# The sparse attention's queries projected transposed: the weight block stationary, 256 tokens moving

## The chip, the core and the metric

The kernel runs on one NeuronCore of a Trainium2 chip. The metric is the device time of one execution in microseconds (us); lower is better. Engines: PE is TensorE's matmuls, PEld its weight loads (the loading of the stationary operand), DVE is VectorE, ACT ScalarE, POOL GpSimd, SP the engine that issues the transfers.

## The reference

One layer of a decoder trunk over 256 tokens of width 2048, all in float32: a pre-norm, one projection of 2048 to 18,776 columns, three token mixers, their gates, a branch projection and an output projection each, and a post-norm with the residual. What matters here is the third mixer:

```python
h = rmsnorm(x, pre_norm_g[l])
proj = jnp.einsum('bsd,dn->bsn', h, w_in[l])       # dsa_q: 8 heads x 256 columns of it
...
q = q.reshape(b, s, DSA_HEADS, DSA_LATENT)         # 8 x 256
c = rmsnorm(ckv, kv_norm_g)
...
logits = jnp.einsum('bqhc,bqkc->bqhk', qb, c_sel).astype(jnp.float32) * (DSA_LATENT ** -0.5)
p = jax.nn.softmax(jnp.where(valid[:, :, None, :], logits, -jnp.inf), axis=-1)
ob = jnp.einsum('bqhk,bqkc->bqhc', p.astype(c.dtype), c_sel)
return jnp.einsum('bqhc,hcv->bqhv', ob, w_uv)
```

The logits contract over the 256 latent columns, so on TensorE the queries have to stand with these columns on the partitions: transposed.

## The kernel before

**Products.** Each float32 operand of a big projection is split in two float32r parts, high and low, and a product is three matmuls: high by high, high by low, low by high. The input's parts are `xhi` and `xlo` (128 partitions of the width, 16 blocks `kt`, 256 tokens). The weights come in units of 256 rows by 512 columns: SP loads a unit into one of four slots of `raw`, ACT rounds it to `whi` (L559), DVE subtracts to get `wlo` (L822), PE multiplies. A unit frees its slot for the rounding of the fourth unit behind it. Eight units make a group of 512 output columns.

**`multiply` (L1223 to L1236).** A unit is 12 matmuls: 2 blocks `kt`, 2 blocks `t` of 128 tokens, 3 products. The stationary operand is 128 tokens of `xhi` or `xlo`, the moving one 512 weight columns; the result stands in two PSUM banks, tokens on the partitions, one bank for each `t`. `take_group` on ACT (L562) copies the two banks to `area0` or `area1` and scales each token by its `rstdx`, the pre-norm's factor, which is per partition there.

**Stages, by parts of the stream.** `PS` (small columns, 344 wide), `PA` (8 groups), `PB` (8), `PC` (4 turns of 2 groups), then per branch b a part `PP[b]` of 4 turns of 12 units (8 units of gates, 4 of the branch's projection), `PV` between `PP[0]` and `PP[1]`, and `PO` (4 groups of `w_out`). Turns 0 and 1 of `PC` are the 2048 columns of the sparse attention's queries: 4 groups, 32 units. The mixers' small operations stand at fixed units between the big ones in the same program: the mLSTM in `PC`, the sparse attention in `PP[1]`, two heads a turn, a head at 6 units.

**The order of a head of the sparse attention in `PP[1]`.** POOL copies the head's 256 query columns to `ya_blk`. After unit u = 0 PE transposes them, 4 transposes of 128x128 into `M[0]` (L1462), and ACT copies them to `dsa_qT` (L750). After u = 1 PE computes the logits in plain float32 (L1469: 4 matmuls, in the trace two passes each), and DVE scales them and adds the mask (L1142) and takes the maxima (L1145). ACT takes the exponential (L755) behind its rounding at u = 2, PE transposes the probabilities after u = 3 (L1475) and multiplies them by the values after u = 4 (L1483, L1485).

**Loops.** On each engine the turns of a part are a hardware loop (`Fori`); the units within a turn are written out. The last turn of `PP[2]` and the 32 units of `PO` are written out altogether. Order between engines is by semaphores that count up.

Of the kernel before, what the change touches and what calls it, by code (L numbers as in the profile page):

```python
# [34 lines left out]
ALU = mybir.AluOpType  # L35
# [3 lines left out]
P = 128  # L39
# [108 lines left out]
def build(nc, x, pre_norm_g, w_in, da_lambda, da_norm_g, ml_conv_w, ml_conv_b, ml_gate_b, ml_norm_g,  # L148
          dsa_kv_norm_g, dsa_ik_norm_g, dsa_w_uv, w_branch, w_out, post_norm_g, out):
    with ExitStack() as ctx:  # L150
# [52 lines left out]
        gate_in = tiny[:, 116:132].rearrange("p (t e) -> p t e", t=TILES)  # L203
        forget_t = tiny[:, 156:164].rearrange("p (t h) -> p t h", t=TILES)
        conv_h = tiny[:, 132:142].rearrange("p (a j) -> p a j", a=2)
        wait_carrier = tiny[:, 166:167]
        sqrt_first = tiny[:, 167:168]
        one = tiny[:, 142:143]
# [55 lines left out]
        idx_acc = view(scratch, 2048, 3 * P)  # L264
        select = view(scratch, 768, 3 * P)
        idx_relu = view(room1, 0, 2, 3 * P)
        dsa_q = ya_blk[:, :, :]
        dsa_qT = view(room0, 512, 2, SEQ)
        dsa_pT = view(room1, 512, 3 * P)
        dsa_s = view(scratch, 1152, 3 * P)  # L270
        dsa_sig = view(scratch, 1536, TILES, P)
# [52 lines left out]
                                                          sem("iw_fetched"))  # L324
        idx_fetched, idx_T_psum, iqT_ready = sem("idx_fetched"), sem("idx_T_psum"), sem("iqT_ready")
        idx_scores, idx_relu_ready, idx_added = sem("idx_scores"), sem("idx_relu_ready"), sem("idx_added")
        dsa_fetched, dsa_T_psum, dsa_qT_ready = sem("dsa_fetched"), sem("dsa_T_psum"), sem("dsa_qT_ready")
        dsa_logits, dsa_negmax, dsa_exp = sem("dsa_logits"), sem("dsa_negmax"), sem("dsa_exp")
        dsa_pT_psum, dsa_pT_ready = sem("dsa_pT_psum"), sem("dsa_pT_ready")
        chi_ready, clo_ready, v_taken = sem("chi_ready"), sem("clo_ready"), sem("v_taken")  # L330
# [107 lines left out]
        def _(pool):  # L438
# [92 lines left out]
                fetch_iw(p * 2 + (IW0 + 2))  # L531


            pool.wait_ge(idx_T_psum, IDX_HEADS // 2)
            nc.gpsimd.tensor_copy(dsa_q, area0[:, :, 0:DSA_LATENT]).then_inc(dsa_fetched, 1)
            with pool.Fori(0, DSA_HEADS - 1) as h:
                pool.wait_ge(dsa_T_psum, h + 1)
                nc.gpsimd.tensor_copy(dsa_q, area0[:, :, bass.ds(h * DSA_LATENT + DSA_LATENT, DSA_LATENT)]  # L538
                                      ).then_inc(dsa_fetched, 1)


            pool.wait_ge(end_landed, 48)
            for n, (t, columns) in enumerate(FINAL_POOL):
                pool.wait_ge(y_scaled, n + 1)
# [5 lines left out]
        def _(act):  # L550
# [11 lines left out]
            def take_group(part, i, k_end, bank_pair, to, width=GROUP):  # L562

                act.wait_ge(units_done, part.unit(i, k_end))
                for t in range(TILES):
                    nc.scalar.activation(to[t], stream[bank_pair][t][:, 0:width], ACT.Copy, scale=rstdx[:, t:t + 1]  # L566
                                         ).then_inc(banks_free, 1)

            act.wait_ge(cols_turned, 1)
            nc.scalar.activation(cols[:, :], M[0][:, 0:56], ACT.Copy).then_inc(cols_ready, 1)  # L570
# [88 lines left out]
            nc.scalar.activation(da_ss, da_ss, ACT.Sqrt).then_inc(da_std, 1)  # L659


            with act.Fori(0, PC.turns) as i:
                for v in range(2 * FULL_UNITS):
                    round_unit(PC, i, v)
                    if v == 1:
                        act.wait_ge(ml_T_psum, i + 1)
                        nc.scalar.activation(ml_xT[:, :, ML_CONV - 1:], M[0][:, :].rearrange("p (a s) -> p a s", a=2),
                                             ACT.Copy).then_inc(ml_xT_ready, 1)
                    if v == 4:
                        act.wait_ge(ml_conv, i + 1)  # L670
                        nc.scalar.activation(ml_sT, ml_cT, ACT.Tanh, scale=0.5).then_inc(ml_ts, 1)
                        act.wait_ge(ml_arg, i * 2 + 2)
                        nc.scalar.activation(ml_E, ml_E, ACT.Exp).then_inc(ml_exp, 1)
                    if v == 11:
                        act.wait_ge(ml_gated, i + 1)
                        nc.scalar.activation(ml_to, area1[:, :, bass.ds(i * ML_V + 2 * WIDTH, ML_V)], ACT.Tanh,
                                             scale=0.5).then_inc(ml_toz, 1)
                        nc.scalar.activation(ml_tz, area1[:, :, bass.ds(i * ML_V + 3 * WIDTH, ML_V)], ACT.Tanh,
                                             scale=0.5).then_inc(ml_toz, 1)
                    if v == 3:  # L680
                        act.wait_ge(ya_psum, i + 1)
                        nc.scalar.activation(yhi[:, bass.ds(i * 2, 2), :],
                                             M[2][:, :].rearrange("p (k s) -> p k s", k=2), ACT.Copy
                                             ).then_inc(yhi_ready, 1)
                    if v in (FULL_UNITS - 1, 2 * FULL_UNITS - 1):
                        g = v // FULL_UNITS
                        take_group(PC, i, (g + 1) * FULL_UNITS, (PC.group0 + g) % 2,
                                   [area0[:, t, bass.ds(i * 2 * GROUP + g * GROUP, GROUP)] for t in range(TILES)])
# [54 lines left out]
            with act.Fori(0, PP[1].turns) as i:  # L743
                for v in range(PAIR_UNITS):
                    round_unit(PP[1], i, v)
                    s, u = v // 6, v % 6
                    h = i * 2 + s
                    if u == 0:
                        act.wait_ge(dsa_T_psum, h + 1)
                        nc.scalar.activation(dsa_qT, M[0][:, :].rearrange("p (c s) -> p c s", c=2), ACT.Copy  # L750
                                             ).then_inc(dsa_qT_ready, 1)
                    if u == 2:
                        act.wait_ge(dsa_negmax, h * 2 + 2)
                        for t, a, n in ((0, 0, P), (1, P, 2 * P)):
# [58 lines left out]
        def _(dve):  # L813
# [60 lines left out]
            steps.step(nc.vector.tensor_tensor(neglam, lam2[:, 1:2], lam2[:, 0:1], ALU.subtract))  # L874
            steps.step(nc.vector.tensor_scalar(neglam, neglam, LAM_INIT, None, ALU.subtract))

            dve.wait_ge(kv_squared, 2)
            steps.step(nc.vector.tensor_reduce(sskv[:, 0:2], kv_sq, AX.X, ALU.add))
            steps.step(nc.vector.tensor_reduce(sskv[:, 2:4], ik_sq, AX.X, ALU.add))
# [254 lines left out]
            with dve.Fori(0, PP[1].turns) as i:  # L1134
                steps.enter(i, 2 * 4)
                for v in range(PAIR_UNITS):
# [2 lines left out]
                    h = i * 2 + s  # L1139
                    if u == 1:  # L1140
                        dve.wait_ge(dsa_logits, h + 1)
                        steps.step(nc.vector.scalar_tensor_tensor(dsa_s, M[1][:, 0:3 * P], DSA_LATENT ** -0.5, select,  # L1142
                                                                  ALU.mult, ALU.add))
                        for t, a, n in ((0, 0, P), (1, P, 2 * P)):
                            nc.vector.tensor_reduce(dsa_negmax_c[:, t:t + 1], dsa_s[:, a:a + n], AX.X, ALU.max,  # L1145
                                                    negate=True).then_inc(dsa_negmax, 1)
# [74 lines left out]
        def _(pe):  # L1221
            def multiply(part, i, k, u, units, bank_pair, left_hi, left_lo, width=GROUP):

                slot = (part.unit0 + k) % RING
                pe.wait_ge(wlo_ready, part.unit(i, k) + 1)
                for j in range(UNIT_KT):
                    kt = UNIT_KT * u + j
                    first, final = kt == 0, kt == UNIT_KT * units - 1
                    for t in range(TILES):
                        to = stream[bank_pair][t][:, 0:width]  # L1230
                        tokens = slice(t * P, (t + 1) * P)
                        high, low = whi[:, slot, j, 0:width], wlo[:, slot, j, 0:width]
                        nc.tensor.matmul(to, left_hi[:, kt, tokens], high, start=first, stop=False)  # L1233
                        nc.tensor.matmul(to, left_hi[:, kt, tokens], low, start=False, stop=False)  # L1234
                        last = nc.tensor.matmul(to, left_lo[:, kt, tokens], high, start=False, stop=final)  # L1235
                last.then_inc(units_done, 1)  # L1236

            def open_banks(part, i, k):
# [103 lines left out]
            last.then_inc(rows_turned, 1)  # L1342


            with pe.Fori(0, PC.turns) as i:
                for v in range(2 * FULL_UNITS):
                    g, u = v // FULL_UNITS, v % FULL_UNITS
                    if u == 0:
                        open_banks(PC, i, g)
                    multiply(PC, i, v, u, FULL_UNITS, (PC.group0 + g) % 2, xhi, xlo)  # L1350
# [23 lines left out]
                    if v == 10:  # L1374
# [6 lines left out]
                        nc.tensor.matmul(M[3][:, 0:n], ml_w[:, P:2 * P], ml_v[:, 0, :], start=True, stop=False)  # L1381
                        nc.tensor.matmul(M[3][:, 0:n], ml_w[:, 2 * P:], ml_v[:, 1, :], start=False, stop=True
                                         ).then_inc(ml_num, 1)

            def gate_units(part, i, v, n0):

# [59 lines left out]
            pe.wait_ge(v_taken, 2)  # L1446


            with pe.Fori(0, PP[1].turns) as i:
                for v in range(PAIR_UNITS):  # L1450
                    s, u = v // 6, v % 6
                    h = i * 2 + s
# [1 line left out]
                        gate_units(PP[1], i, v, 4)  # L1454
                    else:
                        branch_units(PP[1], i, v, 4, 9)
                    if u == 0:
                        pe.wait_ge(dsa_fetched, h + 1)
                        pe.wait_ge(ylo_ready, 9)
                        for c in range(2):  # L1460
                            for t in range(TILES):
                                last = nc.tensor.transpose(M[0][:, c * SEQ + t * P:c * SEQ + (t + 1) * P],  # L1462
                                                           dsa_q[:, t, c * P:(c + 1) * P], ident[:, :])
                        last.then_inc(dsa_T_psum, 1)
                    if u == 1:
                        pe.wait_ge(dsa_qT_ready, h + 1)
                        for t, a, n in ((0, 0, P), (1, P, 2 * P)):
                            for c in range(2):
                                last = nc.tensor.matmul(M[1][:, a:a + n], dsa_qT[:, c, t * P:(t + 1) * P],  # L1469
                                                        cT[:, c, 0:n], start=(c == 0), stop=(c == 1))  # L1470
                        last.then_inc(dsa_logits, 1)
                    if u == 3:
# [84 lines left out]
```

## Time and profile before

| | before |
|---|---|
| device time, 3 runs | median 1133.67 us (1132.83 to 1134.2) |
| span of the profiled execution | 1131.5 us |
| PE busy, matmuls | 1110.0 us, 98% of the span |
| PEld busy | 915.0 us, 81% |
| DVE, ACT, POOL busy | 657.7, 549.5, 70.8 us |
| chain that ended last | 95% on PE |
| mean granted clock of TensorE | 0.995 of full speed |

The span runs from the first to the last instruction; of the profiled execution it is the only time there is, and the median of the timed runs is 2.2 us above it. A PE record lasts longer than the engine needs for it: records of matmuls that follow each other overlap, so the distance from start to start is what a matmul costs. The start of a weight load coincides with the start of the matmul before it, so starts of weight loads tell when matmuls begin.

### The profile page before, as it was taken

Reading aid. Unit: us, or ns where it says so; the run is one execution under the profiler, and the core shown is the slowest. Engines: PE = TensorE matmul, PEld = TensorE weight load, DVE = VectorE, ACT = ScalarE, POOL = GpSimd, SP = SyncE. Lnnn points to the kernel's source line nnn. Section 1 sums busy time; section 2 is a strip of 40 time slices with the busy share of each in tenths; the row PEclk is TensorE's granted clock in tenths of the full one; section 3 lists DMA queues with packets and bytes.
Section 4 is the critical chain, followed back from the end, with each engine's and each line's share of the span. In section 5 each row is a group of like instructions: output and inputs, shape, how many; then the busy total and the mean of one; then the engine's idle time right before and its main releaser. Section 6 shows DMA issues by size and latency. Waiting matters only on the chain.

```text
span 1131.5 us, 15625 instructions
## 1 busy us (share of the span) xinstructions
PE 1110.0 (98%) x5143; PEld 915.0 (81%) x5143; DVE 657.7 (58%) x910; ACT 549.5 (49%) x736; POOL 70.8 (6%) x122
## 2 busy tenths in 40 slices
PE   7999999999999999999999999999999999999995
PEld 6788888888878888888887778888888888888884
DVE  4744444666566676665766566665556645556454
ACT  6644444555454554544546444454444544445442
POOL 1000000100100011120210000000000000000001
PEclk9999999999999999999999999999999999999998
DMA  8666666566556546666556556655555476676551
GB/s 245 223 190 192 197 188 197 173 170 183 167 169 175 167 140 184 192 180 184 169 168 192 164 157 191 205 167 163 166 163 160 129 222 191 197 238 229 196 195 75
DMA packets 112399, 205.09 MB, mean 181 GB/s; under 512 B 11064, under 2 KB 15728, under 8 KB 111984
## 3 DMA queue, kind: packets, MB, share of 16 engines
q1 hardware_dynamic: 112368, 204.70, 60.1%
q8 instruction: 17, 0.28, 0.1%
q14 instruction: 14, 0.11, 0.0%
HBM read 202.57 MB, written 2.10 MB: 181 GB/s over the span
## 4 chain that ended last, share of the span: by engine, by line
PE 95%; SPq 2%; DVE 1%; ACT 1%; issue 0%; DMA 0%; DVEq 0%; ACTq 0%
PE stream L1233 30%; PE stream L1235 30%; PE stream L1234 29%; SPq L367 1%; PE mixer L1469 1%; DVE area L1216 1%; DVE wlo L822 0%; PE mixer L1496 0%; PE mixer L1485 0%; PE mixer L1328 0%; PE mixer L1303 0%; PE mixer L1404 0%; PE mixer L1462 0%; PE mixer L1429 0%; PE mixer L1314 0%
## 5 line engine op out<-in xcount | busy, mean ns | idle before, releaser
L822 DVE TENSOR_TENSOR wlo<-raw,whi 128x1024 fp32r<-128x1024 f32 (+1 forms) x378 | 460.9, 1222 | 430.5 <-ACT whi L559 428.5
L559 ACT ACTIVATE whi<-raw 128x1024 fp32r<-128x1024 f32 (+1 forms) x378 | 397.7, 1054 | 553.6 <-PE stream L1235 537.9
L1233 PE MATMUL stream<-whi,xhi 128*128 128x512 f32 (+1 forms) x1312 | 518.6, 395 | 2.8 <-DVE wlo L822 2.4
L1235 PE MATMUL stream<-whi,xlo 128*128 128x512 f32 (+1 forms) x1312 | 510.1, 389 | 0.0
L1234 PE MATMUL stream<-wlo,xhi 128*128 128x512 f32 (+1 forms) x1312 | 509.0, 388 | 0.0
L1233 PEld LDWEIGHTS stream<-whi,xhi 128*128 128x128 f32 x1312 | 246.8, 188 | 56.6 <-issue 5.8
L1235 PEld LDWEIGHTS stream<-whi,xlo 128*128 128x128 f32 x1312 | 246.6, 188 | 51.6
L1234 PEld LDWEIGHTS stream<-wlo,xhi 128*128 128x128 f32 x1312 | 247.1, 188 | 48.1
L1233 PE MATMUL stream<-whi,yhi 128*128 128x512 f32 x192 | 77.1, 401 | 0.0
L1235 PE MATMUL stream<-whi,ylo 128*128 128x512 f32 x192 | 75.0, 391 | 0.0
L1234 PE MATMUL stream<-wlo,yhi 128*128 128x512 f32 x192 | 74.8, 390 | 0.0
L1235 PEld LDWEIGHTS stream<-whi,ylo 128*128 128x128 f32 x192 | 36.0, 188 | 7.8
L1233 PEld LDWEIGHTS stream<-whi,yhi 128*128 128x128 f32 x192 | 36.1, 188 | 7.6 <-issue 0.7
L1234 PEld LDWEIGHTS stream<-wlo,yhi 128*128 128x128 f32 x192 | 36.1, 188 | 7.1
L566 ACT ACTIVATE area<-stream,tiny 128x512 f32 x48 | 30.0, 675 | 0.0
L468 POOL COPY mixed<-area 128x256 f32 (+1 forms) x24 | 10.7, 467 | 193.7 <-ACT area L566 173.6
L546 POOL TENSOR_TENSOR area<-area 128x512 f32<-128x512 f32 x3 | 5.0, 1696 | 261.6 <-ACT area L808 261.6
L538 POOL COPY ya_blk<-area 128x512 f32 x7 | 4.3, 612 | 190.8 <-PE mixer L1462 190.8
L697 ACT ACTIVATE area<-stream,tiny 128x512 f32<-128x512 f32 x24 | 15.0, 677 | 0.0
L472 POOL TENSOR_TENSOR mixed<-mixed 128x256 f32<-128x256 f32 x8 | 4.9, 614 | 159.2 <-DVE mixed L954 159.2
L637 ACT ACTIVATE mixed<-mixed,tiny 128x128 f32<-128x128 f32 (+1 forms) x32 | 14.1, 441 | 0.0
L513 POOL TENSOR_TENSOR mixed<-mixed 128x512 f32<-128x512 f32 x4 | 7.8, 1953 | 87.4 <-DVE mixed L1031 87.4
(244 smaller groups left out, 567.9 us busy)
## 6 DMA issues: line engine op xcount, KB each, us to landing
raw<-in_w_in SPq DMA_DIRECT2D x288, 512.0 KB, 3.7
raw<-in_w_branch SPq DMA_DIRECT2D x48, 512.0 KB, 4.5
raw<-in_w_out SPq DMA_DIRECT2D x32, 512.0 KB, 3.7
mixed<-in_x SPq DMA_DIRECT2D x4, 512.0 KB, 6.0
raw<-in_w_in SPq DMA_DIRECT2D x8, 256.0 KB, 3.9
area<-in_x SPq DMA_DIRECT2D x2, 1024.0 KB, 9.2
out<-area SPq DMA_DIRECT2D x8, 256.0 KB, 2.3
raw<-in_dsa_w_uv SPq DMA_DIRECT2D x4, 256.0 KB, 3.0
```

The source lines that it names most:

```text
L367: sp.dma_start(raw[:, slot, :, at:at + n], w_in_d[:, UNIT_KT * u:UNIT_KT * (u + 1), col:col + n]).then_inc(raw_landed[slot], 16)
L468: nc.gpsimd.tensor_copy((da_q, da_k, da_v)[n], area0[:, :, bass.ds(at + n * WIDTH, P)]).then_inc(da_v_fetched if n == 2 else da_fetched, 1)
L559: nc.scalar.activation(whi[:, slot, :, 0:width], raw[:, slot, :, 0:width], ACT.Copy).then_inc(whi_ready, 1)
L566: nc.scalar.activation(to[t], stream[bank_pair][t][:, 0:width], ACT.Copy, scale=rstdx[:, t:t + 1]).then_inc(banks_free, 1)
L637: nc.scalar.activation(da_s[:, c, a:a + n], da_s[:, c, a:a + n], ACT.Exp, bias=da_negmax_c[:, 2 * t + c:2 * t + c + 1], accum_out=da_sum_c ...
L697: nc.scalar.activation(sig[:, t, :], stream[part.group0 % 2][t][:, :], ACT.Tanh, scale=half_rstdx[:, t:t + 1]).then_inc(gate_tanh, 1)
L822: nc.vector.tensor_tensor(wlo[:, slot, :, 0:width], raw[:, slot, :, 0:width], whi[:, slot, :, 0:width].bitcast(F32), ALU.subtract).then_in ...
L1216: nc.vector.scalar_tensor_tensor(to, to, rstdo[:, t:t + 1], x_again[:, t, columns], ALU.mult, ALU.add).then_inc(y_dve, 1)
L1233: nc.tensor.matmul(to, left_hi[:, kt, tokens], high, start=first, stop=False)
L1234: nc.tensor.matmul(to, left_hi[:, kt, tokens], low, start=False, stop=False)
L1235: last = nc.tensor.matmul(to, left_lo[:, kt, tokens], high, start=False, stop=final)
L1469: last = nc.tensor.matmul(M[1][:, a:a + n], dsa_qT[:, c, t * P:(t + 1) * P], cT[:, c, 0:n], start=(c == 0), stop=(c == 1))
```

## The change

In turns 0 and 1 of `PC` the operands change places. A new `multiply_turned` takes 128 weight columns as the stationary operand and all 256 tokens as the moving one, so that the result stands transposed: latent columns on the partitions, tokens along the free axis. A unit is then 24 matmuls of 256 columns in place of 12 of 512. One bank holds one head, each half of it one block of 128 of its latent columns. `take_group` copies these banks unscaled (a token is no longer a partition), and `dsa_qT` is the copy in `area0` itself. The factor `rstdx` goes into the scaling of the logits on DVE, as `rstd_q` (with the 1/16 of the logits), one instruction for each block of tokens in place of one for both. POOL's copies to `ya_blk`, PE's transposes and ACT's copies for them go, with the three semaphores between them. On PE and ACT the body of `PC` is written out twice, for turns 0 and 1 and for turns 2 and 3, and PE's loop over the turns of `PP[1]` is written out.

```diff
+        rstd_q = tiny[:, 164:166]
...
-        dsa_q = ya_blk[:, :, :]
-        dsa_qT = view(room0, 512, 2, SEQ)
+        dsa_qT = [area0[:, h % 2, h // 2 * GROUP:(h // 2 + 1) * GROUP].rearrange("p (c s) -> p c s", c=2)
+                  for h in range(DSA_HEADS)]
...
-            pool.wait_ge(idx_T_psum, IDX_HEADS // 2)
-            nc.gpsimd.tensor_copy(dsa_q, area0[:, :, 0:DSA_LATENT]).then_inc(dsa_fetched, 1)
-            with pool.Fori(0, DSA_HEADS - 1) as h:
-                pool.wait_ge(dsa_T_psum, h + 1)
-                nc.gpsimd.tensor_copy(dsa_q, area0[:, :, bass.ds(h * DSA_LATENT + DSA_LATENT, DSA_LATENT)]
-                                      ).then_inc(dsa_fetched, 1)
...
-                    nc.scalar.activation(to[t], stream[bank_pair][t][:, 0:width], ACT.Copy, scale=rstdx[:, t:t + 1]
-                                         ).then_inc(banks_free, 1)
+                    nc.scalar.activation(to[t], stream[bank_pair][t][:, 0:width], ACT.Copy,
+                                         scale=1.0 if turned else rstdx[:, t:t + 1]).then_inc(banks_free, 1)
...
+            with act.Fori(0, 2) as i:
+                mlstm_turn(i, True)
+            with act.Fori(2, PC.turns) as i:
+                mlstm_turn(i, False)
...
-                    if u == 0:
-                        act.wait_ge(dsa_T_psum, h + 1)
-                        nc.scalar.activation(dsa_qT, M[0][:, :].rearrange("p (c s) -> p c s", c=2), ACT.Copy
-                                             ).then_inc(dsa_qT_ready, 1)
...
+            steps.step(nc.vector.tensor_scalar(rstd_q, rstdx, DSA_LATENT ** -0.5, None, ALU.mult))
             dve.wait_ge(kv_squared, 2)
...
-                        steps.step(nc.vector.scalar_tensor_tensor(dsa_s, M[1][:, 0:3 * P], DSA_LATENT ** -0.5, select,
-                                                                  ALU.mult, ALU.add))
+                        for t, a, n in ((0, 0, P), (1, P, 2 * P)):
+                            last = nc.vector.scalar_tensor_tensor(dsa_s[:, a:a + n], M[1][:, a:a + n],
+                                                                  rstd_q[:, t:t + 1], select[:, a:a + n],
+                                                                  ALU.mult, ALU.add)
+                        steps.step(last)
...
+            def multiply_turned(part, i, k, u, bank_pair):
+
+                slot = (part.unit0 + k) % RING
+                pe.wait_ge(wlo_ready, part.unit(i, k) + 1)
+                for j in range(GROUP // P):
+                    columns = slice(j * P, (j + 1) * P)
+                    to = stream[bank_pair][j // 2][:, j % 2 * SEQ:(j % 2 + 1) * SEQ]
+                    for c in range(UNIT_KT):
+                        kt = UNIT_KT * u + c
+                        high, low = whi[:, slot, c, columns], wlo[:, slot, c, columns]
+                        nc.tensor.matmul(to, high, xhi[:, kt, :], start=kt == 0 and j % 2 == 0, stop=False,
+                                         skip_group_check=True)
+                        nc.tensor.matmul(to, high, xlo[:, kt, :], start=False, stop=False, skip_group_check=True)
+                        last = nc.tensor.matmul(to, low, xhi[:, kt, :], start=False, stop=kt == KT - 1,
+                                                skip_group_check=True)
+                last.then_inc(units_done, 1)
...
-            with pe.Fori(0, PP[1].turns) as i:
+            for i in range(PP[1].turns):
...
-                    if u == 0:
-                        pe.wait_ge(dsa_fetched, h + 1)
+                    if u == 1:
                         pe.wait_ge(ylo_ready, 9)
-                        for c in range(2):
-                            for t in range(TILES):
-                                last = nc.tensor.transpose(M[0][:, c * SEQ + t * P:c * SEQ + (t + 1) * P],
-                                                           dsa_q[:, t, c * P:(c + 1) * P], ident[:, :])
-                        last.then_inc(dsa_T_psum, 1)
-                    if u == 1:
-                        pe.wait_ge(dsa_qT_ready, h + 1)
                         for t, a, n in ((0, 0, P), (1, P, 2 * P)):
                             for c in range(2):
-                                last = nc.tensor.matmul(M[1][:, a:a + n], dsa_qT[:, c, t * P:(t + 1) * P],
+                                last = nc.tensor.matmul(M[1][:, a:a + n], dsa_qT[h][:, c, t * P:(t + 1) * P],
                                                         cT[:, c, 0:n], start=(c == 0), stop=(c == 1))
```

## Rows read from the trace of the kernel before

**Rows 1.** The page: busy time of two engines, and the granted clock in 40 slices.

```profile
PE 1110.0 (98%) x5143; PEld 915.0 (81%) x5143; DVE 657.7 (58%) x910; ACT 549.5 (49%) x736; POOL 70.8 (6%) x122
PEclk9999999999999999999999999999999999999998
```

**Rows 2.** Waits of PE: who was waited for, us in total, times, longest.

```profile
PE stream L1233 <- DVE wlo L822: 2.4, 4, 1.2
```

**Rows 3.** Weight loads in order of time, 344 columns moving: start, duration; 40 records.

```profile
23.84 0.19 PEld L1235 LDWEIGHTS stream<-whi,xlo 128*128 128x128 f32 x1
...
29.82 0.19 PEld L1235 LDWEIGHTS stream<-whi,xlo 128*128 128x128 f32 x1
```

**Rows 4.** Weight loads, 512 columns moving: 12 records from 30.66, 36 from 33.21.

```profile
30.55 0.19 PEld L1233 LDWEIGHTS stream<-whi,xhi 128*128 128x128 f32 x1 [0.55 <-DVE wlo L822]
30.66 0.19 PEld L1234 LDWEIGHTS stream<-wlo,xhi 128*128 128x128 f32 x1
...
33.21 0.19 PEld L1233 LDWEIGHTS stream<-whi,xhi 128*128 128x128 f32 x1
...
41.14 0.19 PEld L1235 LDWEIGHTS stream<-whi,xlo 128*128 128x128 f32 x1
```

**Rows 5.** Weight loads around a head's transposes of the queries (L1462) in `PP[1]`.

```profile
744.04 0.59 PEld L1462 LDWEIGHTS mixer<-ident,ya_blk 128*128 128x128 f32 x4
...
744.71 0.19 PEld L1234 LDWEIGHTS stream<-wlo,xhi 128*128 128x128 f32 x1
```

**Rows 6.** Chain that ended last: the transposes of the first and the last of 8 heads.

```profile
744.43 0.44 PE mixer L1462 x4
...
879.09 0.44 PE mixer L1462 x4
```

**Rows 7.** Weight loads around the other three blocks of the first head.

```profile
747.23 1.29 PEld L1469 LDWEIGHTS mixer<-scratch,area 128*128 128x128 f32 x8
...
748.77 0.19 PEld L1234 LDWEIGHTS stream<-wlo,xhi 128*128 128x128 f32 x1
...
754.03 0.47 PEld L1475 LDWEIGHTS mixer<-ident,scratch 128*128 128x128 f32 x3
...
754.59 0.19 PEld L1234 LDWEIGHTS stream<-wlo,xhi 128*128 128x128 f32 x1
...
757.11 0.41 PEld L1483 LDWEIGHTS mixer<-area 128*128 128x128 f32 x2
757.45 0.53 PEld L1485 LDWEIGHTS mixer<-area 128*128 128x128 f32 x4
757.89 0.19 PEld L1233 LDWEIGHTS stream<-whi,xhi 128*128 128x128 f32 x1
758.00 0.19 PEld L1234 LDWEIGHTS stream<-wlo,xhi 128*128 128x128 f32 x1
```

**Rows 8.** Weight loads in `PO`, whose program is written out: 44 records.

```profile
1059.82 0.19 PEld L1233 LDWEIGHTS stream<-whi,xhi 128*128 128x128 f32 x1
...
1069.56 0.19 PEld L1234 LDWEIGHTS stream<-wlo,xhi 128*128 128x128 f32 x1
```

**Rows 9.** DVE and ACT around the new instruction's place: start, duration.

```profile
37.88 0.17 DVE L881 TENSOR_SCALAR tiny<-tiny 128x2 f32<-128x2 f32 x1
...
37.95 1.28 ACT L603 ACT_TABLE_LOAD   x1
39.24 0.21 ACT L603 ACTIVATE tiny<-tiny 128x4 f32<-128x4 f32 x1
```

**Rows 10.** DVE and ACT of the first head, between the logits and the exponential.

```profile
749.88 0.55 DVE L1142 SCALAR_TENSOR_TENSOR scratch<-mixer,scratch 128x384 f32<-128x384 f32 x1
750.47 0.61 DVE L1145 TENSOR_REDUCE tiny<-scratch 128x1 f32<-128x128 f32 x2
...
752.70 0.38 ACT L755 ACTIVATE scratch<-scratch,tiny 128x128 f32<-128x128 f32 x1
```

More of the change, by code:

```diff
@@ L326, in build @@
         idx_scores, idx_relu_ready, idx_added = sem("idx_scores"), sem("idx_relu_ready"), sem("idx_added")
-        dsa_fetched, dsa_T_psum, dsa_qT_ready = sem("dsa_fetched"), sem("dsa_T_psum"), sem("dsa_qT_ready")
         dsa_logits, dsa_negmax, dsa_exp = sem("dsa_logits"), sem("dsa_negmax"), sem("dsa_exp")
@@ L560, in round_unit, with take_group @@
                                      ).then_inc(whi_ready, 1)
-            def take_group(part, i, k_end, bank_pair, to, width=GROUP):
+            def take_group(part, i, k_end, bank_pair, to, width=GROUP, turned=False):
                 act.wait_ge(units_done, part.unit(i, k_end))
                 for t in range(TILES):
-                    nc.scalar.activation(to[t], stream[bank_pair][t][:, 0:width], ACT.Copy, scale=rstdx[:, t:t + 1]
-                                         ).then_inc(banks_free, 1)
+                    nc.scalar.activation(to[t], stream[bank_pair][t][:, 0:width], ACT.Copy,
+                                         scale=1.0 if turned else rstdx[:, t:t + 1]).then_inc(banks_free, 1)
             act.wait_ge(cols_turned, 1)
@@ L659, in _, with mlstm_turn @@
             nc.scalar.activation(da_ss, da_ss, ACT.Sqrt).then_inc(da_std, 1)
-            with act.Fori(0, PC.turns) as i:
+            def mlstm_turn(i, turned):
                 for v in range(2 * FULL_UNITS):
@@ L687, in _ @@
                         take_group(PC, i, (g + 1) * FULL_UNITS, (PC.group0 + g) % 2,
-                                   [area0[:, t, bass.ds(i * 2 * GROUP + g * GROUP, GROUP)] for t in range(TILES)])
+                                   [area0[:, t, bass.ds(i * 2 * GROUP + g * GROUP, GROUP)] for t in range(TILES)],
+                                   turned=turned)
+            with act.Fori(0, 2) as i:
+                mlstm_turn(i, True)
+            with act.Fori(2, PC.turns) as i:
+                mlstm_turn(i, False)
             act.wait_ge(ml_ms, 1)
@@ L1342, in _, with mlstm_turn @@
             last.then_inc(rows_turned, 1)
-            with pe.Fori(0, PC.turns) as i:
+            def mlstm_turn(i, turned):
                 for v in range(2 * FULL_UNITS):
@@ L1349, in _ @@
                         open_banks(PC, i, g)
-                    multiply(PC, i, v, u, FULL_UNITS, (PC.group0 + g) % 2, xhi, xlo)
+                    if turned:
+                        multiply_turned(PC, i, v, u, (PC.group0 + g) % 2)
+                    else:
+                        multiply(PC, i, v, u, FULL_UNITS, (PC.group0 + g) % 2, xhi, xlo)
                     if v == 1:
@@ L1383, in _ @@
                                          ).then_inc(ml_num, 1)
+            with pe.Fori(0, 2) as i:
+                mlstm_turn(i, True)
+            with pe.Fori(2, PC.turns) as i:
+                mlstm_turn(i, False)
             def gate_units(part, i, v, n0):
```

## The prediction

> **What bounds the kernel now.** First the page: PE is busy 98% of the span, DVE 58%, ACT 49%, and the granted clock is at its full level in all but the last slice [rows 1]. A busy PE is not yet a bound, so next the waits of PE: behind the start, all waiting for the rounded weights comes to 2.4 us in four places [rows 2]. PE is thus never starved from some 43 us on, and the time is the sum of what PE is given to do. What an operation costs there is not its record (0.19 us for a weight load) but the distance between starts. With 512 columns moving that is (41.14 - 33.21)/35 = 0.2266 us [rows 4], with 344 columns (29.82 - 23.84)/39 = 0.1533 us [rows 3]. The change is to be priced in such distances, all on PE.
>
> **What it removes on PE.** Eight blocks of four transposes. Around the first head's block, the matmul before it begins at 744.04 and the first matmul behind it at 744.71 (the load for the one after starts with it) [rows 5]. That is 0.67 us less one stream matmul: 0.443 us. The chain of work gives the same 0.44 [rows 6]. Eight of them: 3.54 us.
>
> A block also interrupts the stream, and that has a price of its own. Heads repeat every (879.09 - 744.43)/7 = 19.24 us [rows 6]. In this lie 72 stream matmuls, 72 x 0.2266 = 16.31, the logits 1.54 - 0.23 = 1.31, the transposes of the probabilities 0.56 - 0.23 = 0.33, and the product with the values 0.89 - 0.23 = 0.66 [rows 7], with the queries' 0.44 a total of 19.05. The missing 0.18 us lie behind the four interruptions, 0.045 each. One is seen after the wait at 30.55: for 11 matmuls the distance is 0.2318 before it settles at 0.2266, 0.057 in all [rows 4]. Eight interruptions fewer at 0.045: 0.36 us. Removed together: 3.9 us. From below, if the tails belong to the other blocks alone, 3.5; from above, with 0.057 each, 4.0.
>
> **What it adds on PE.** 32 units of 24 matmuls with 256 columns moving replace 32 of 12 with 512: 768 for 384. The old ones cost 384 x 0.2266 = 87.0 us. No row has a float32r matmul of 256 columns. Two limits stand for it.
>
> The moving side: through the rows at 344 and 512 the slope is 0.0733/168 = 0.436 ns a column with 3.4 ns left over, so 256 columns take 115.0 ns. Lower bound: the cost goes with the columns alone, as if no fixed part existed, 0.2266/2 = 113.3 ns. Upper bound: 344 columns at 2.4 GHz (the clock is at its upper level in these stretches) are 143.3 ns, so 10 ns lie over; if all of them are fixed, 106.7 + 10 = 116.7 ns.
>
> The weight side: the number of loads doubles, and each still loads 128 columns. How long does one really take? Behind the wait the load starts at 30.55 and its matmul at 30.66 [rows 4]: 0.11 us, with nothing else in the array. Behind the product with the values, which are passes of full 128x128 loads, the starts of the last five passes are 757.45 to 757.89, 0.11 each, and the stream's own first load takes until 758.00, again 0.11 [rows 7]. So a load can be repeated every 0.11 us, and 115 ns of matmul cover it, by only 5 ns. At 512 columns the cover was more than 100 ns.
>
> The Trainium skill ("TensorE: Matmul & The Clock Gate", section "LDWEIGHTS (loading the stationary operand)") has a load at its columns over 1.2, for 128 an estimated 107 ns whatever the rows; the trace's 0.11 agrees, and not the record's 0.19. The same page's "Back-to-back issue gap" gives load-and-matmul pairs sustained 81 ns at 128 columns and 131 at 512; a straight line between them is 98 at 256, two of which cost 64 ns more than one of 512, an estimate of 384 x 0.064 = 25 us against this change. The trace does not bear those figures out: its 512 columns take 227 ns, so I don't go by them; what they warn of is the second rival.
>
> I take 115.0 ns, the line through the two nearest rows: 768 x 0.1150 = 88.3 us, 1.3 us more than before. Bounds from the moving side: 87.0 (nothing) and 89.6 (2.6 more).
>
> **What costs nothing, and why.**
> - *The 16 interruptions of the mLSTM* in turns 0 and 1 of the projection stay where they are.
> - *The scale `rstd_q` on DVE*, early: one tiny operation like L881, 0.17 us and its step. DVE finishes L881 at 38.05, ACT is then loading a table until 39.23 and takes the root behind it at 39.24 [rows 9]. The 0.2 us fall into that 1.2. Without this cover the rounded weights, for which PE waits at this place [rows 2], would come 0.2 us later and so would the end.
> - *Two scalings of the logits in place of one*, some 0.2 us more for the second's overhead: L1142 ends at 750.43, the maxima near 751.1, and ACT's exponential starts at 752.70 behind its own rounding [rows 10]. 1.6 us cover it. Uncovered, the transposes of the probabilities, which PE begins one matmul after 754.03 [rows 7], would come late, by 8 x 0.2 = 1.6 us at most.
> - *ACT's and POOL's copies*, 16 in all: neither engine is waited for, so their going gives nothing. `take_group` has the same two copies with another scale.
> - *PE's wait for `ylo_ready`* goes from behind unit 0 to behind unit 1, a place later, with nothing queued ahead of it that it could hold.
> - *Written-out code*: in `PO`, where PE's program is written out, (1069.56 - 1059.82)/43 = 0.2265 us [rows 8], the same as in loops; and the eight starts of the transposes are evenly 19.24 us apart, whether the end of a turn lies between them or not [rows 6]. Neither a gain nor a loss.
> - *Transfers*: SP's list is the same, and no queue is moved past.
>
> **The sum.** -3.9 + 1.3 = -2.6 us. The profiled span of 1131.5 us becomes 1128.9; the median stands 2.2 us above that span, so 1133.67 - 2.6 = 1131.1 us, 0.23% less. What this kernel's measurement can tell from no change is about 0.2%, 2.3 us, so the forecast stands just over that line.
>
> **The rivals.**
> *First, a fixed part per matmul, still under the old time.* Price: 116 to 118 ns each, all fixed or with a few ns of the load uncovered. Speaks for it: the load's 0.11 us has only 5 ns of cover, and behind each interruption the stream runs 5 ns a matmul slower for a while [rows 4]. Time: 768 x 0.117 = 89.9, +2.9, so -1.0: 1132.7 us, no difference that can be told.
>
> *Second, the load becomes the bound.* If a load at 0.11 us has to hand over to its matmul with what a matmul of 512 columns has over its columns, 226.6 - 213.3 = 13.3 ns, the distance is 123.3 ns: 768 x 0.1233 = 94.7, +7.7, less 3.9 is +3.8: 1137.5 us, slower. It cancels the gain from 118.4 ns on, (87.0 + 3.9)/768, and is measurably slower from 121.3. Against it: the passes of 128 columns repeat every 0.11 with a full load each, so no handing over shows there [rows 7]. Were even the record of 0.19 us the true cost, the price would be 768 x 0.075 = 57 us; but at 344 columns a matmul starts every 0.153 [rows 3], so that is excluded.
>
> *Third, no fixed part at all:* 113.3 ns, and the change keeps its whole 3.9 us: 1129.8 us.
>
> *Fourth, the queries' time comes back as a wait:* with the block gone, PE could reach the probabilities' transposes before the exponential is done. It begins at 752.70, its first half takes 0.38 us [rows 10], and PE comes at 754.26 [rows 7]. But ACT starts it behind a rounding that waits for PE's own unit u = 2, so both move together. With the 1.6 us above as its price it would be 1132.7 us; I count it in with the first.
>
> **How the numbers follow.** Forecast (114 to 116 ns) 0.42, third 0.13, first 0.27, second 0.18. The first three share -3.9 to -0.5 us. Faster by over 0.2% takes a time under 1131.4: the third and most of the forecast, 0.50. Slower by over 0.2% takes 121.3 ns: 0.14 of the second's 0.18. Same: 0.36. Range: from the third rival's 1129.6 to 1135.5, which is 120.7 ns; above it about one in seven is left. The likeliest's own range is 1130.0 to 1132.0.
>
> **What would show it.** In the trace after, in the first two turns of the stage at 410 to 500 us: starts of weight loads 0.115 us apart, the stage 1.3 us longer than before. Distances of 0.117 and more, or a matmul that idles between loads, speak for the first two rivals. In the sparse attention the period of a head is 18.75 us in place of 19.24, with three interruptions. PE's waits stay at 2.4 us for the rounded weights; if they grow, one of the covers above was gone. Wrong I would be by the one price that no row shows, the distance at 256 columns: each nanosecond of it is 0.77 us.

## The result: 0.1% slower, where 0.2% faster was forecast

| | before | changed |
|---|---|---|
| device time, median of 20 runs | 1133.01 us | 1134.28 us |
| lowest and highest | 1131.52, 1135.2 | 1132.8, 1138.03 |
| span of the profiled execution | 1131.5 us | 1131.3 us |

The ratio is 1.0014, with a 95% interval of 1.0008 to 1.0021: within the 0.2% that were named as the limit of what can be told, but on the other side of 1 than forecast, and its interval leaves 1 out; in time it is +1.3 us, and 0.9 to 2.4 by the interval. Timed again beside other kernels, the changed one had 1.0008 (0.9999 to 1.0017), 12 runs.

The two profiled spans are no measure of it: the changed kernel's is even shorter (why is told under its second profile). So the profile is read by stages. First the page of the changed kernel, and its waits of PE (who was waited for, us in total, times, longest):

```profile
PE 1109.6 (98%) x5495; PEld 931.9 (82%) x5495; DVE 658.2 (58%) x919; ACT 542.1 (48%) x726; POOL 63.8 (6%) x114
PE stream L1231 <- DVE wlo L816: 1.9, 2, 1.3
```

PE is the bound as before and waits no more than it did [rows 1, 2]. The covers held, then. What counts is what PE is given to do. Weight loads in order of time, in turn 0 of the queries' projection; the rows left out are 163 more at the same distance:

```profile
440.44 0.19 PEld L1246 LDWEIGHTS stream<-xhi,whi 128*128 128x128 f32 x1
...
460.12 0.19 PEld L1249 LDWEIGHTS stream<-xhi,wlo 128*128 128x128 f32 x1
```

165 loads are 164 distances: 19.68/164 = 0.1200 us, where 0.1150 was taken. Then the chain of work, the logits of the first and last head:

```profile
750.73 1.31 PE mixer L1484 x8
...
882.11 1.31 PE mixer L1484 x8
```

The period of a head is (882.11 - 750.73)/7 = 18.77 us, against 19.24 [rows 6]; 18.75 was forecast.

### The profile page after: what moved, and what is told of

Its sections match the earlier page's. It is cut to its first block, busy times and chain, and to the rows that moved or that the text cites. A ratio compares the mean times of both kernels' runs of the same rounds, so it can differ in the third digit from the quotient of the medians.

```text
span 1131.3 us, 16192 instructions
## 1 busy us (share of the span) xinstructions
PE 1109.6 (98%) x5495; PEld 931.9 (82%) x5495; DVE 658.2 (58%) x919; ACT 542.1 (48%) x726; POOL 63.8 (6%) x114
## 4 chain that ended last, share of the span: by engine, by line
PE 96%; DVE 2%; DMA 1%; ACT 0%; issue 0%; SPq 0%; DVEq 0%; ACTq 0%
PE stream L1231 28%; PE stream L1233 27%; PE stream L1232 27%; PE stream L1246 3%; PE stream L1249 3%; PE stream L1248 3%; PE mixer L1484 1%; DVE wlo L816 1%; DMA mixed<-in_x 1%; DVE area L1214 1%; PE mixer L1511 0%; PE mixer L1500 0%; PE mixer L1343 0%; PE mixer L1318 0%; PE mixer L1427 0%; PE mixer L1452 0%
## 5 line engine op out<-in xcount | busy, mean ns | idle before, releaser
L1231 PE MATMUL stream<-whi,xhi 128*128 128x512 f32 (+1 forms) x1184 | 466.8, 394 | 2.3 <-DVE wlo L816 1.9
L1233 PE MATMUL stream<-whi,xlo 128*128 128x512 f32 (+1 forms) x1184 | 459.8, 388 | 0.0
L1232 PE MATMUL stream<-wlo,xhi 128*128 128x512 f32 (+1 forms) x1184 | 459.4, 388 | 0.0
L1232 PEld LDWEIGHTS stream<-wlo,xhi 128*128 128x128 f32 x1184 | 223.0, 188 | 43.2
L1246 PE MATMUL stream<-xhi,whi 128*128 128x256 f32 x256 | 73.4, 287 | 0.0
L1249 PE MATMUL stream<-xhi,wlo 128*128 128x256 f32 x256 | 72.4, 283 | 0.0
L1248 PE MATMUL stream<-xlo,whi 128*128 128x256 f32 x256 | 72.4, 283 | 0.0
L1248 PEld LDWEIGHTS stream<-xlo,whi 128*128 128x128 f32 x256 | 48.8, 191 | 0.1
L1246 PEld LDWEIGHTS stream<-xhi,whi 128*128 128x128 f32 x256 | 48.8, 191 | 0.1
L1249 PEld LDWEIGHTS stream<-xhi,wlo 128*128 128x128 f32 x256 | 48.8, 191 | 0.0
```

The source lines that it names most:

```text
L1246: nc.tensor.matmul(to, high, xhi[:, kt, :], start=kt == 0 and j % 2 == 0, stop=False, skip_group_check=True)
L1248: nc.tensor.matmul(to, high, xlo[:, kt, :], start=False, stop=False, skip_group_check=True)
L1249: last = nc.tensor.matmul(to, low, xhi[:, kt, :], start=False, stop=kt == KT - 1, skip_group_check=True)
```

## The experiments

All are compared with the kernel before on the same chip. "Distance" is from start to start of the weight loads.

### Two of 256 in place of one of 512, without turning anything

```diff
-                        to = stream[bank_pair][t][:, 0:width]
                         tokens = slice(t * P, (t + 1) * P)
-                        high, low = whi[:, slot, j, 0:width], wlo[:, slot, j, 0:width]
...
+                        for piece in range(pieces):
+                            part_of = slice(piece * width // pieces, (piece + 1) * width // pieces)
+                            to = stream[bank_pair][t][:, part_of]
+                            high, low = whi[:, slot, j, part_of], wlo[:, slot, j, part_of]
...
```

`pieces` is 2 in all four turns of `PC` and 1 elsewhere.

> The kernel before, but all four turns of the mLSTM's part (64 units) do each matmul of 512 columns as two of 256 with the same roles as before: tokens stationary, weights moving. Nothing is turned. If the width alone sets the cost (each matmul of 256 takes 120.0 ns, whichever operand moves): 1536 x 0.1200 - 768 x 0.2266 = 184.3 - 174.0 = +10.3 us on the kernel before, about 1143.3 us, ratio 1.0091. Rival, that the cost comes from the exchanged roles (weights stationary out of the ring that ACT and DVE write): 115.0 ns here, +2.6 us, 1135.6 us, ratio 1.002.

Measured: 1143.31 us, ratio 1.0087 (1.0074 to 1.01), where the theory had 1143.3 and 1.0091. Weight loads of this kernel, 159 records:

```profile
442.13 0.19 PEld L1237 LDWEIGHTS stream<-whi,xhi 128*128 128x128 f32 x1
...
461.09 0.19 PEld L1241 LDWEIGHTS stream<-whi,xlo 128*128 128x128 f32 x1
```

(461.09 - 442.13)/158 = 0.1200 us, with the old roles. The price hangs on the width, not on which operand moves. By the chain a turn of this stage takes 48.88 us, where the kernel before takes 46.53: 9.4 us in four turns, and not quite the 10.3 of the sum. What is missing is told below, under the turned stage; the interval of the timed runs (8.4 to 11.4 us) holds both.

### The changed kernel with the multiplication unturned

```diff
                     if turned:
-                        multiply_turned(PC, i, v, u, (PC.group0 + g) % 2)
+                        multiply(PC, i, v, u, FULL_UNITS, (PC.group0 + g) % 2, xhi, xlo)
```

> The changed kernel with the one part undone that costs: in turns 0 and 1 TensorE multiplies as before (tokens stationary, 512 weight columns moving), all else stays as changed, so the sparse attention gets its queries untransposed and its values are others than the reference's. Theory (the gain is the predicted one, the matmuls of 256 cost 120.0 ns): 768 x 0.1200 - 87.0 = 5.2 us less than the changed kernel, 3.8 to 3.9 less than the kernel before: about 1129.2 us, ratio 0.9966. Rival (the transposes' time came back elsewhere and the matmuls cost 115 to 117 ns): at most 2.6 us less than the changed kernel, 1131.7 us or more, ratio 0.9985 or above.

Measured: 1128.41 us, ratio 0.9956 (0.9943 to 0.9968); expected 0.9966, inside the interval. The head's period is the changed kernel's, 18.77 us. What this kernel computes is not the reference's attention. With the expensive half undone, the gain of the other half is there, and not smaller than forecast; the rival falls.

### Turned, but 512 tokens' columns moving

```diff
-                    to = stream[bank_pair][j // 2][:, j % 2 * SEQ:(j % 2 + 1) * SEQ]
-                    for c in range(UNIT_KT):
-                        ...
-                        nc.tensor.matmul(to, high, xhi[:, kt, :], start=kt == 0 and j % 2 == 0, stop=False,
-                        ...
+                    to = stream[bank_pair][j // 2][:, :].rearrange("p (c s) -> p c s", c=2)
+                    both = slice(UNIT_KT * u, UNIT_KT * (u + 1))
+                    high, low = whi[:, slot, j % 2, columns], wlo[:, slot, j % 2, columns]
+                    nc.tensor.matmul(to, high, xhi[:, both, :], start=u == 0 and j % 2 == 0, stop=False,
...
```

> The changed kernel with the roles exchanged but 512 columns moving: 128 weight columns stationary, two blocks of 256 tokens moving at once, 12 matmuls a unit in place of 24. Half of the products are left out and the others summed differently, so the queries are not the reference's. If the width sets the cost: 0.2266 us a matmul in turns 0 and 1, the same time as with the multiplication unturned, about 1129.2 us, ratio 0.9966. If the roles set it: more than 0.2266 us a matmul; at 0.240 it would be 384 x 0.0134 = 5.2 us more, 1134.3 us.

Measured: 1130.08 us, ratio 0.9971 (0.996 to 0.9981), expected 0.9966. 34 weight loads:

```profile
442.34 0.19 PEld L1248 LDWEIGHTS stream<-xhi,wlo 128*128 128x128 f32 x1
...
449.83 0.19 PEld L1248 LDWEIGHTS stream<-xhi,wlo 128*128 128x128 f32 x1
```

7.49/33 = 0.227 us, as unturned. The exchanged roles cost nothing.

### TensorE alone: which width, which load

Two programs in which TensorE has nothing but matmuls to do, each run once. The first had all groups on one line, and its starts could not be told apart; only its groups' busy times can be read.

> The disputed cost by itself: a program that does none of the reference's work but copies x to the output, and has TensorE run groups of 48 float32r matmuls, each with its own load of 128 columns, moving 512, 448, 384, 344, 320, 288, 256, 192 and 128 columns; then 256 and 512 into two banks in turn, and 256 with loads of 64 and of 32 columns. Theory A (every float32r matmul has a fixed part of 13.3 ns whatever its width, as 120.0 - 106.7 and 226.6 - 213.3 suggest): 200 ns at 448, 173 at 384, 133 at 288, 120 at 256, and it goes on falling to 93 at 192 and 67 at 128; shorter loads change nothing at 256. Theory B (the load of 128 columns can be repeated only every 120 ns in this stream, and bounds at 256): 120 ns at 256, 192 and 128 alike, and at 256 with loads of 64 or 32 columns it falls to 115 or less. If what costs is adding up in one bank time after time, two banks in turn are faster than one; neither theory expects it.

Measured, as (busy time less one record)/47: 0.147 at 320 columns, 0.157 at 344, 0.111 at 192 and at 128, and at 256 with loads of 64 or of 32 columns 0.113. Neither theory: it stops falling at 0.111, not at 0.120 (against B), and 256 gets cheaper with a short load (against A). So a second program, with a line for each group.

> TensorE alone again, none of the reference's work: 16 groups of 48 float32r matmuls, each group on its own line. Moving 512, 344, 288, 256, 192 and 128 columns, with loads of 128, 96, 64 and 32 columns; 256 also into two banks in turn, and with the same stationary block every time. Theory A+ (a load of 128 columns beside a matmul costs it 13.3 ns at every width from 256 up, shorter loads cost it less, and below some 230 columns the load itself bounds at 0.111 us): 226.7, 156.7, 133.3 and 120.0 ns at 512, 344, 288 and 256 with loads of 128; about 113.3 at 256 and 220 at 512 with loads of 64 or 32; 111 at 192 and at 128 with loads of 128, and lower with loads of 32. Rival (13.3 ns belong to the matmul, the load is innocent; 256 with short loads in the earlier program was an artefact of overlapping records): 120.0 at 256 with every load. Two banks or the same block change nothing in either.

Its matmuls in order of time (start, then the time all 48 take together, line, rows and columns of the load with an asterisk between, columns moving); the distance of two starts over 48 is the cost of one:

```profile
34.38 11.04 PE L60 MATMUL bank<-whi 128*128 128x512 f32 x48
45.26 11.20 PE L62 MATMUL bank<-whi 128*64 128x512 f32 x48
56.30 11.28 PE L64 MATMUL bank<-whi 128*32 128x512 f32 x48
67.42 7.74 PE L66 MATMUL bank<-whi 128*128 128x344 f32 x48
75.00 7.68 PE L68 MATMUL bank<-whi 128*32 128x344 f32 x48
82.51 6.48 PE L70 MATMUL bank<-whi 128*128 128x288 f32 x48
88.83 5.92 PE L72 MATMUL bank<-whi 128*128 128x256 f32 x48
94.58 5.92 PE L74 MATMUL bank<-whi 128*128 128x256 f32 x48
100.34 5.73 PE L76 MATMUL bank<-whi 128*96 128x256 f32 x48
105.91 5.61 PE L78 MATMUL bank<-whi 128*64 128x256 f32 x48
111.36 5.60 PE L80 MATMUL bank<-whi 128*32 128x256 f32 x48
116.80 5.92 PE L82 MATMUL bank<-whi 128*128 128x256 f32 x48
122.56 5.50 PE L84 MATMUL bank<-whi 128*128 128x192 f32 x48
127.90 4.40 PE L86 MATMUL bank<-whi 128*32 128x192 f32 x48
132.14 5.49 PE L88 MATMUL bank<-whi 128*128 128x128 f32 x48
137.47 3.04 PE L90 MATMUL bank<-whi 128*32 128x128 f32 x48
```

| moving | load 128 | 96 | 64 | 32 |
|---|---|---|---|---|
| 512 | 226.7 ns | | 230.0 | 231.7 |
| 344 | 157.9 | | | 156.5 |
| 288 | 131.7 | | | |
| 256 | 119.8 (two banks 120.0, same block 120.0) | 116.0 | 113.5 | 113.3 |
| 192 | 111.3 | | | 88.3 |
| 128 | 111.0 | | | 59 (from the group's own time) |

At 128 and 192 columns the load of 128 bounds, at 0.111 us. At 256 a matmul with the shortest load takes 113.3, half of 226.7, and the load of 128 adds 6.7, although 111 is less than 113. At 512 the full load adds nothing; short ones are even slower there, by 3 and 5 ns. So the rival falls (256 is not 120.0 with every load), and of theory A+ its middle: "13.3 ns at every width" is not what the loads cost. Two banks and the same block change nothing.

### The same in the kernel: loads of 64 beside 256 columns

```diff
-                        tokens = slice(t * P, (t + 1) * P)
+                        rows_of = P // pieces
+                        tokens = slice(t * P, t * P + rows_of)
...
```

The cut is on top of the halves above. Half of the tokens' results are left out with it.

> The kernel with the halves (all four turns of the mLSTM's part with matmuls of 256 columns, tokens stationary), but each load has 64 tokens in place of 128, so that half of the tokens' results are left out; the number and width of the matmuls stay. Theory (at 256 columns 6.7 of the 13.3 ns over the columns belong to the load of 128, as in the program with TensorE alone: 113.5 ns with a load of 64): 1536 x 0.1134 - 768 x 0.2266 = +0.2 us on the kernel before, ratio 1.000, and 10 us less than with the halves and full loads. Rival (the loads are innocent in the kernel, the width costs): 120.0 ns, +10.3 us, ratio 1.009.

Measured: 1132.46 us, ratio 0.9988 (0.9979 to 0.9997); expected 1.000. 90 weight loads:

```profile
441.90 0.14 PEld L1240 LDWEIGHTS stream<-wlo,xhi 128*64 128x64 f32 x1
...
451.99 0.13 PEld L1238 LDWEIGHTS stream<-whi,xhi 128*64 128x64 f32 x1
```

10.09/89 = 0.1134 us. The same number and width of matmuls as with the halves, only the loads shorter, and all of that kernel's 10 us is gone. The ratio is 0.1% under the expected one. By the chain a turn takes 46.44 us against 46.53 before, 0.4 us less in four turns, where the sum has 0.2 more: this accounts for a part of it, and the rest lies within the interval.

### A head's four transposes put back

```diff
+                    if u == 0:
+                        pe.wait_ge(ylo_ready, 9)
+                        for c in range(2):
+                            for t in range(TILES):
+                                nc.tensor.transpose(M[0][:, c * SEQ + t * P:c * SEQ + (t + 1) * P],
+                                                    dsa_qT[h][:, c, t * P:(t + 1) * P], ident[:, :])
...
```

> The changed kernel with one cost of the kernel before put back: after unit 0 of each head TensorE again does four transposes of 128x128 into the first mixer bank, here of the already transposed queries, and nobody reads them (so the output is the reference's, but nothing waits for ACT's or POOL's copies). Theory (a block costs 0.44 us on TensorE and its interruption 0.03 to 0.05, and nothing else was in the way): 8 x 0.47 to 0.49 = 3.8 to 3.9 us more than the changed kernel, near 1138.1 us, and the head's period is 19.24 us again. Rival (part of the gain came from copies and waits that are gone): less than 3 us more, and a period under 19.15.

Measured: 1138.36 us, 3.81 more than the changed kernel on the same chip (1134.55). The chain has a block at 750.55 and its seventh successor at 885.34:

```profile
750.55 0.44 PE mixer L1484 x4
...
885.34 0.44 PE mixer L1484 x4
```

A period of 19.26 us. The blocks account for all that the change gains; the copies on POOL and ACT, and the waits for them, had cost nothing.

### The blocks beside another block

```diff
                         last.then_inc(dsa_out, 1)
+                        if h < DSA_HEADS - 1:
+                            turn_q(h + 1)
...
```

`turn_q` is the four transposes; they stand behind the product with the values.

> The kernel before with its queries untouched, but TensorE transposes the queries of head h + 1 right behind head h's product with the values, in place of a unit later, so that seven of the eight blocks no longer interrupt the stream by themselves. Theory (an interruption costs 0.03 to 0.05 us beside the block itself): 7 x 0.04 = 0.3 us less, a head's period of 19.19 to 19.20 us in place of 19.24; ratio 0.9997, not to be told from no change by the timed runs. Rival (interruptions cost nothing, the missing time lay elsewhere): the period stays at 19.24.

Measured: 1133.07 us, ratio 0.9996 (0.9987 to 1.0005). The logits in the chain:

```profile
746.79 1.31 PE mixer L1472 x8
...
880.95 1.31 PE mixer L1472 x8
```

The period is 134.16/7 = 19.17 us, 0.07 less than before, where 0.04 to 0.05 was expected. An interruption does cost by itself. It has the lowest ratio of the changed kernels that compute all of the reference, but 0.4 us is not to be told from no change by timing.

### The changed kernel once more

> The changed kernel as it is, timed on the same chip as the others and profiled once more. Both theories: +1.3 us on the kernel before, ratio 1.001. In its profile the starts of weight loads in turns 0 and 1 stand 0.120 us apart. Open is the stretch behind the matmuls with 4 rows at 404 us: the kernel before ran about 3.3 us at the lower clock there (1.6 us lost), the changed kernel's profile did not; if that is chance it may well show here.

Measured: 1134.55 us, ratio 1.0008 (0.9999 to 1.0017); span of the profile 1133.2 us. Its loads behind the matmuls with 4 rows, in turn 0:

```profile
406.31 0.27 PEld L1246 LDWEIGHTS stream<-xhi,whi 128*128 128x128 f32 x1
...
406.89 0.33 PEld L1246 LDWEIGHTS stream<-xhi,whi 128*128 128x128 f32 x1
407.10 0.33 PEld L1248 LDWEIGHTS stream<-xlo,whi 128*128 128x128 f32 x1
...
409.45 0.33 PEld L1246 LDWEIGHTS stream<-xhi,whi 128*128 128x128 f32 x1
```

12 distances from 406.89 to 409.45, 0.213 us each in place of 0.120: here, too, the clock is at its lower level for some 3.3 us. It was so in the kernel before, and not in the first profile of the changed one, as the granted clock by stage tells (us, busy time and number of each engine, clock, transfers); the kernel before, then the changed kernel's first profile, then its second:

```profile
404.50:410.00 5.50, 5.50 (x21) 4.37 (x21) 3.74 (x13) 4.42 (x9) 2.66 (x8) 0.69 0.37 114
```

```profile
404.50:410.00 5.50, 5.50 (x45) 5.30 (x44) 3.74 (x11) 4.71 (x10) 2.65 (x8) 1.00 0.52 158
```

```profile
404.50:410.00 5.50, 5.50 (x32) 5.24 (x31) 3.74 (x10) 4.73 (x9) 2.64 (x8) 0.69 0.54 176
```

Of the nine profiles of whole kernels six have this stretch and three have not; the one kernel profiled twice has it once, so it does not hang on the program alone. All three without it have a stretch at the lower clock near 17 us instead (0.66 to 0.71 between 15 and 20 us), but the one with halved loads has both; what decides is open. It takes 1.5 to 1.6 us, by the stage lengths below. With it the first two spans can be added up by the chain: PE's own chain began 0.6 us later in the changed kernel (43.55 against 42.97), the turned stage took 4.7 us more but was spared these 1.6, and the heads took 3.8 less. That makes -0.1, and the spans differ by -0.2.

## Why the prediction was wrong

The forecast was -2.6 us, measured is +1.3 (from the medians). Step by step:

- **The transposes and their interruptions: right.** Forecast -3.9; by the heads' periods 8 x (19.24 - 18.77) = -3.8, by putting them back 3.81.
- **The matmuls of 256 columns: the term that was mis-sized.** The step that failed is "I take 115.0 ns, the line through the two nearest rows"; they cost 120.0. That is 768 x 0.1200 - 87.0 = +5.2 us in place of +1.3, and it turns the sign of the sum. The upper bound, "if all of them are fixed, 106.7 + 10 = 116.7 ns", was no bound.
- **The turned stage as a whole: +4.7, not +5.2.** The chain times it, from the block of 8 before the first turned unit to the first block of turn 2. The changed kernel's first profile, then the one with the blocks beside another, whose projection is unchanged; neither has the stretch at the lower clock:

```profile
403.57 1.92 PE mixer L1350 x8
...
509.10 0.44 PE mixer L1373 x4
```

```profile
403.84 1.92 PE mixer L1335 x8
...
504.70 0.44 PE mixer L1355 x4
```

  105.53 against 100.86 us: 4.67 more. With the stretch the changed kernel's second profile has 107.01 (403.93 to 510.94) and the kernel before 102.45 (403.00 to 505.45): 4.56 more. The half microsecond under 5.2 lies behind the interruptions, which the prediction let "stay where they are". Behind the first block of turn 0, in the changed kernel and then unturned:

```profile
411.91 0.19 PEld L1248 LDWEIGHTS stream<-xlo,whi 128*128 128x128 f32 x1
...
413.11 0.19 PEld L1249 LDWEIGHTS stream<-xhi,wlo 128*128 128x128 f32 x1
```

```profile
411.91 0.19 PEld L1234 LDWEIGHTS stream<-wlo,xhi 128*128 128x128 f32 x1
...
414.23 0.19 PEld L1235 LDWEIGHTS stream<-whi,xlo 128*128 128x128 f32 x1
```

  Ten distances each: 0.120 us with 256 columns, nothing over, and 0.232 with 512, where the stream settles at 0.2266. So the tail of 0.05 us behind each interruption is gone in the turned stage. There are 8 blocks in it, 4 a turn (the prediction's 16 are those of all four turns), and one before it: 9 x 0.05 = 0.5 us. The sum is then -3.8 + 4.7 = +0.9 us, at the lower end of what the timed runs allow (0.9 to 2.4, and -0.1 to 1.9 when timed again).
- **Why the line failed.** It went through a row at 344 columns and one at 512, out to 256. The row at 344 was one execution's: 0.1533 us. In the changed kernel's profile the same loads (38 of them) read

```profile
24.34 0.19 PEld L1232 LDWEIGHTS stream<-wlo,xhi 128*128 128x128 f32 x1
...
30.18 0.19 PEld L1233 LDWEIGHTS stream<-whi,xlo 128*128 128x128 f32 x1
```

  which is 5.84/37 = 0.1578 us; the experiments' profiles of whole kernels have 0.158 there too, and the program with TensorE alone has 0.1579. Why the one execution had 0.1533 stays open. A line from 344 to 512 carries an error at 344 to 256 one and a half times: with 0.158 it would have given 122 ns, and no gain.
- **The load as bound: half seen.** The 0.11 us were right (111 ns measured), and 5 ns of cover were called thin. But I took the dearer of matmul and load as the cost. At 256 columns the cost is neither 113 nor 111 but 120; the load adds 6.7 ns, which the kernel shows by itself when the loads are halved. The second rival had named the right direction; its 13.3 ns, put on the 106.7 of the columns in place of the load, would give 120.0, but that would be luck: at 256 columns the 13.3 are 6.6 of the matmul and 6.7 of the load, and at 512 the load has no part in them. Through what the load and the matmul get in each other's way at 256, and not at 512, the runs don't show. The Trainium skill's figures for sustained pairs of load and matmul ("TensorE: Matmul & The Clock Gate", "Back-to-back issue gap"), 81 ns at 128 columns and 131 at 512, warned in the right direction, but they don't fit this stream: at the same widths it takes 111 and 226.7 ns.
- **The clock: read too coarsely.** The prediction had it at its full level in all but the last slice. A digit 9 means 90% or more and a slice is 28 us wide, so the 3.3 us at the lower clock did not show in the row. It did not enter the sum, but it is worth more than the measured effect.
- **The covers: right.** The scale `rstd_q` made ACT's root no later: DVE's last operation for it now ends at 38.84, ACT's table is there at 39.82. From DVE's operation on the gates to the reciprocal behind the root it is 5.66 us in both kernels (33.82 to 39.48, 34.41 to 40.07). The two scalings of the logits take 0.74 us in place of 0.55, and the maxima are done 1.4 us before the exponential:

```profile
38.67 0.17 DVE L876 TENSOR_SCALAR tiny<-tiny 128x2 f32<-128x2 f32 x1
38.54 1.28 ACT L595 ACT_TABLE_LOAD   x1
752.99 0.74 DVE L1138 SCALAR_TENSOR_TENSOR scratch<-mixer,tiny,scratch 128x128 f32<-128x128 f32 x2
753.76 0.61 DVE L1143 TENSOR_REDUCE tiny<-scratch 128x1 f32<-128x128 f32 x2
755.81 0.38 ACT L749 ACTIVATE scratch<-scratch,tiny 128x128 f32<-128x128 f32 x1
```

- **Written-out code, copies, waits: right**, they gave and took nothing that shows.

So the change pays where a head's 96 matmuls of 256 columns cost less over its 48 of 512 than the block they save: here 4.7/8 = 0.58 us against 0.47. By this sum turning fewer heads does not help, since both go with the number of heads. The break-even is (87.0 + 3.8 + 0.5)/768 = 118.9 ns a matmul, where the prediction had 118.4.

## What to carry to other kernels

Where TensorE is the bound, price matmuls by the distance of their starts at the very width, and don't reach a new width by a line through two others out of one execution: 4.5 ns at 344 columns turned the sign here. Halving the moving width doubles the loads, and a load that just fits under its matmul isn't free: leave it well covered, or measure it first in a program of a few lines. Turning an operand in the projection is worth it when the transposes it saves cost more than 12 to 13 ns for each two matmuls of 256 that replace one of 512.

## What was not expected of the hardware

- With 512 columns moving, a load of 32 or 64 columns made the matmul 3 to 5 ns slower than a load of 128. The 231.7 ns of the shortest is near the 0.232 us behind an interruption; whether the two are one thing no run shows.
- At the lower clock level neither a fixed part nor the load shows: 0.213 us at 256 columns is 256/1.2, nothing over.
- An interruption of the stream of 512 columns costs 0.04 to 0.07 us beside the block itself; with 256 columns moving and full loads the stream shows no such tail.
- A stretch of some 3.3 us at the lower clock, behind eight passes with 4 rows and four small transposes, is there in one execution of a kernel and missing in another: 1.5 to 1.6 us, more than the whole effect under study.
